# Sharing out the projection steps beside the attention by the number of keys of a unit

## The reference, cut to what matters

```python
proj = x @ w_in[l]                       # 1024 x 1024 tokens and channels, all branches' columns
q, k, v = ...                            # 8 heads of 64 channels
logf = jax.nn.log_sigmoid(c_f + b_forget[l])
cum = jnp.cumsum(logf, axis=1).transpose(0, 2, 1)
for i in range(seq // Q_BLOCK):          # 8 blocks of 128 queries
    q0, end = i * Q_BLOCK, (i + 1) * Q_BLOCK
    s = jnp.einsum('bqhd,bkhd->bhqk', q[:, q0:end], k[:, :end]) * scale
    s = jnp.where(causal, s + decay, -jnp.inf)
    p = jax.nn.softmax(s, axis=-1)
    outs.append(jnp.einsum('bhqk,bkhd->bqhd', p, v[:, :end]))
```

## Time and profile before

| what | value |
|---|---|
| median of 3 runs | 1223.13 us (1222.97 to 1225.02) |
| the profiled execution: its own time | 1223.87 us |
| the profiled execution: span in the trace | 1222.1 us |
| TensorE (PE) busy | 1203.0 us, 98% of the span, 5704 matmuls |
| VectorE (DVE) busy | 781.5 us, 64% |
| GpSimd (POOL) busy | 693.5 us, 57% |
| ScalarE (ACT) busy | 539.5 us, 44% |
| the four attention pairs | from 644.5 to about 935 us of the span |
| chain that ended last | PE 86%, DVE 7%, ACT 3%, issue 2%, DMA 1%, POOL 1% |

### The profile page before, as it was taken

One profiled execution on the slowest core, in us unless ns is written; L12 is line 12 of the kernel. 1 busy time (PEld: TensorE's weight loads), 2 busy tenths in 40 slices (PEclk: granted clock), 3 DMA queues, 4 the chain that ended last, 5 costly groups with the idle time before them and its releaser, 6 DMA issues.

```text
span 1222.1 us, 15758 instructions
## 1 busy us (share of the span) xinstructions
PE 1203.0 (98%) x5704; PEld 999.2 (82%) x5704; DVE 781.5 (64%) x1285; ACT 539.5 (44%) x992; POOL 693.5 (57%) x550
## 2 busy tenths in 40 slices
PE   7999999999999999999999999999999999999997
PEld 6888888888888888888888888888888888878886
DVE  4723765677566674438587665666666786876755
ACT  5433434344443443557354565656556444315000
POOL 5677887887777777777226444455533225547000
PEclk9999999999999999999999999999999999999999
DMA  8022131232323423234412111111002533376131
GB/s 278 1 69 69 35 104 35 69 138 101 106 105 103 138 104 104 104 105 148 162 53 56 32 53 52 35 53 46 24 18 92 191 111 116 105 260 241 66 130 69
DMA packets 91277, 118.61 MB, mean 97 GB/s; under 512 B 6072, under 2 KB 72632, under 8 KB 91200
## 3 DMA queue, kind: packets, MB, share of 16 engines
q1 hardware_dynamic: 91200, 117.60, 29.2%
HBM read 92.39 MB, written 25.20 MB: 96 GB/s over the span
## 4 chain that ended last, share of the span: by engine, by line
PE 86%; DVE 7%; ACT 3%; issue 2%; DMA 1%; POOL 1%; DVEq 0%; SPq 0%; ACTq 0%
PE pj L745 11%; PE pj L746 11%; PE pj L747 11%; PE pj L816 5%; PE pj L817 5%; PE pj L818 5%; PE pj L1074 4%; PE pt L746 3%; PE pt L747 3%; PE pt L745 3%; PE po L930 3%; PE pt L917 2%; PE po L1074 2%; PE pt L1074 2%; PE pj L833 2%
## 5 line engine op out<-in xcount | busy, mean ns | idle before, releaser
L1571 POOL TENSOR_TENSOR ring_lo<-w_pair,ring_hi 128x512 fp32r<-128x512 f32 x168 | 232.3, 1385 | 111.3 <-ACT ring_hi L1130 111.1
L1624 POOL TENSOR_TENSOR w_lo<-w_raw,w_hi 128x128 fp32r<-128x128 f32 (+1 forms) x104 | 111.2, 1088 | 161.6 <-ACT w_hi L1220 159.5
L1130 ACT ACTIVATE ring_hi<-w_pair 128x512 fp32r<-128x512 f32 x168 | 105.1, 628 | 160.6 <-PE pj L747 108.6
L1785 DVE SCALAR_TENSOR_TENSOR po<-glu,cwa,po 128x512 f32<-128x512 f32 x232 | 159.4, 747 | 20.6 <-ACT po L1181 20.6
L745 PE MATMUL pj<-t_hi,ring_hi 128*128 128x512 f32 x392 | 152.8, 390 | 0.3 <-DVE slot L1749 0.3
L746 PE MATMUL pj<-t_lo,ring_hi 128*128 128x512 f32 x392 | 152.5, 389 | 0.0
L747 PE MATMUL pj<-t_hi,ring_lo 128*128 128x512 f32 x392 | 152.5, 389 | 0.0
L816 PE MATMUL pj<-xT_hi,w_hi 128*128 128x512 f32 x320 | 126.5, 395 | 0.0
L817 PE MATMUL pj<-xT_lo,w_hi 128*128 128x512 f32 x320 | 125.4, 392 | 0.0
L818 PE MATMUL pj<-xT_hi,w_lo 128*128 128x512 f32 x320 | 125.0, 391 | 0.0
L1664 POOL TENSOR_SCALAR probs<-probs,rinv 128x128 f32<-128x128 f32 (+3 forms) x32 | 57.9, 1810 | 110.8 <-DVE rinv L2103 110.8
(11 more groups left out here) (344 smaller groups left out, 2952.1 us busy)
## 6 DMA issues: line engine op xcount, KB each, us to landing
w_pair<-in_w_in SPq DMA_DIRECT2D x28, 1024.0 KB, 5.2
gate_scratch<-slot SPq DMA_DIRECT2D x16, 1024.0 KB, 4.0
gate<-gate_scratch SPq DMA_DIRECT2D x32, 512.0 KB, 3.8
w_raw<-in_w_in SPq DMA_DIRECT2D x20, 512.0 KB, 3.9
z_scratch<-slot SPq DMA_DIRECT2D x8, 512.0 KB, 2.6
bias<-cum_scratch SPq DMA_DIRECT2D x8, 512.0 KB, 3.8
wout_raw<-in_w_out SPq DMA_DIRECT2D x8, 512.0 KB, 5.5
x_tok<-in_x SPq DMA_DIRECT2D x8, 512.0 KB, 4.3
```

What stands on the lines that cost most here:

```text
L1130: nc.scalar.activation(ring_hi[:, j % RING, :, :], w_src(u, p), ACT.Copy).then_inc(s_rhi, 1)
L1571: nc.gpsimd.tensor_tensor(ring_lo[:, j % RING, :, :], w_src(u, p), ring_hi[:, j % RING, :, :], ALU.subtract).then_inc(s_rlo, 1)
L1624: nc.gpsimd.tensor_tensor(w_lo[:, j % 2, k, :], w_raw[:, j % 2, k, :], w_hi[:, j % 2, k, :], ALU.subtract).then_inc(s_wlo, 1)
L1785: nc.vector.scalar_tensor_tensor(out=acc if n < PAD_A else src, in0=src, scalar=cwa[:, ct, n:n + 1], in1=acc, op0=ALU.mult, op1=ALU.add).t ...
```

## The change

A table gives every unit its number of steps, small where the unit has few keys and large where it has many, the same for both heads of the pair. Everything that was tied to "four steps a unit" is derived from the table: where the steps of a unit begin (FILL_AT), which unit takes out half n (EVAC_AT) and which unit splits the next weight tile (SPLIT_AT).

```diff
+        FILL_N = (2, 3, 3, 4, 4, 5, 5, 6) * 2
+        FILL_AT = [sum(FILL_N[:u]) for u in range(UNITS + 1)]
+        EVAC_AT = [next(u for u in range(UNITS + 1) if FILL_AT[u] >= KT * (n + 1)) for n in range(8)]
+        SPLIT_AT = [next(u for u in range(UNITS + 1) if FILL_AT[u] >= 2 * KT * n) for n in range(4)]
...
             def pair(c, last):
                 s = 4 * c
                 for u in range(UNITS):
-                    cut = 4 * u + (3 if u < 2 else 2)
+                    cut = FILL_AT[u] + (FILL_N[u] + 1) // 2
                     if u == 1:
                         turn_v(c)
-                    stream_part(s + S_C, S_C, 4 * u, cut)
+                    stream_part(s + S_C, S_C, FILL_AT[u], cut)
...
-                    stream_part(s + S_C, S_C, cut, 4 * u + 4)
+                    stream_part(s + S_C, S_C, cut, FILL_AT[u + 1])
...
-                    if k % 4 == 0:
-                        split_w(2 * c, 4 + k // 4)
+                    if k in SPLIT_AT:
+                        split_w(2 * c, 4 + SPLIT_AT.index(k))
...
-                    h = k // 2 % 2 ^ 1
-                    if k in (2, 4):
-                        raw_half(s + 3, h, q_raw, QSCALE)
...
-                    if k == 14:
-                        evac_half(s + 6, 0, 0, ACT.Tanh, 0.5)
+                    if k in EVAC_AT[:7]:
+                        n = EVAC_AT.index(k)
+                        h = n % 2
+                        if n < 2:
+                            raw_half(s + 3, h, q_raw, QSCALE)
...
+                        else:
+                            evac_half(s + 3 + n // 2, h, h, ACT.Tanh, 0.5)
...
-                    if k == 14:
+                    if k == EVAC_AT[6]:
                         gate_half(0, sg, 2 * c + 2 * last)
```

More of the change, by code:

```diff
@@ L1430, in pair @@
                             k_hi(a, range(2 - a))
-                    h = k // 2 % 2 ^ 1
-                    if k in (2, 4):
-                        raw_half(s + 3, h, q_raw, QSCALE)
[L1434 to L1439, removed]
-                    if k == 14:
-                        evac_half(s + 6, 0, 0, ACT.Tanh, 0.5)
+                    if k in EVAC_AT[:7]:
[3 more added lines that the diff above has]
+                            raw_half(s + 3, h, q_raw, QSCALE)
+                        elif n < 4:
+                            raw_half(s + 4, h, k_raw, QSCALE if last else 1.0)
+                        elif n < 6 and not last:
+                            raw_half(s + 5, h, v_raw, 0.5)
+                        else:
+                            evac_half(s + 3 + n // 2, h, h, ACT.Tanh, 0.5)
                 turned_hi(c, UNITS - 1)
@@ L1672, in pair @@
                         normalise(c, k + 1)
-                    if k % 4 == 0:
-                        split_w(4 * c + 4 + k // 4, 4 + k // 4)
+                    if k in SPLIT_AT:
+                        split_w(4 * c + 4 + SPLIT_AT.index(k), 4 + SPLIT_AT.index(k))
                     if k == 2 and c:
@@ L2153, in pair @@
                         q_lo(1, q_raw, q_stack, stk + 2)
-                    h = k // 2 % 2 ^ 1
-                    if k in (10, 12) and last:
-                        gate_half(h, v_raw, 2 * c)
-                    if k == 14:
+                    if k in EVAC_AT[4:6] and last:
+                        gate_half(EVAC_AT.index(k) % 2, v_raw, 2 * c)
+                    if k == EVAC_AT[6]:
                         gate_half(0, sg, 2 * c + 2 * last)
```

## The result

| | before | changed |
|---|---|---|
| median of 6 runs | 1223.34 us (1222.50 to 1225.02) | 1228.77 us (1227.22 to 1229.19) |
| ratio | | 1.0039 [1.0027, 1.0052] |
| profiled execution, its own time | 1223.87 | 1227.22 |
| its span | 1222.1 | 1225.4 |
| attention, start of the first scores to start of the memory's scores | 293.89 | 299.22 |

The changed kernel is slower by 5.4 us, 0.39%. Its profiled execution is the fastest of its runs, so the two spans lie only 3.3 us apart. The stretch that the change touches shows the whole of it. Two rows of TensorE's timeline bound this stretch, first in the kernel before, then in the changed one. A row is: start, length shown, engine, line, instruction, out<-in, tile, shape, count, and in brackets the idle time ahead of it and what ended that.

The account below looks back on a forecast made before the run. TensorE, busy 98% of the span, was taken as the bound, so only its standing counted. Terms -5.4 + 0.3 + 1.1 + 4.2 + 5.1 gave +5.3, a median of 1228.4 us; range 1226.0 to 1231.0, 8 in 10 1222.5 to 1232.0.

Parts of the forecast that it names:

- The sixteen waits go: Units 5, 7, 13 and 15 of all four pairs: `turn` no longer waits for VectorE's rests, -5.4 us.
- Unit 13/14 of the last pair: Last pair: VectorE waits in unit 13 for gate half 5 behind a weight tile's split, +0.3 us once.
- Start of pair 0: Units 0 and 1 lose two steps ahead of the second half of `turn_v`, so TensorE stands there, +1.1 us.
- Boundary: Between pairs, three times: gate half 6 lengthens the ScalarE and VectorE chain to 11.0 us, +1.4 each, +4.2 us.
- Units 1 to 4: Every pair: two fewer steps become standing at `turn` of unit 4, 1.4 in pairs 1 to 3, 0.9 in pair 0, +5.1.
- The scaling at 2.91 us: Unit 4: GpSimd's scaling of 640 columns still takes 2.91 us behind k_lo, against 1.8 alone.
- the light units cost nothing: Rival: the two steps taken from units 1 to 4 weren't needed; sum +0.2, 1223.3 us; chance 0.16.
- The chain at the boundary has play: Rival: gate half slips in at +0.4 each and units 1 to 4 close up; -2.8, 1220.3 us; chance 0.09.
- More places turn late: Rival: slack in units 11 and 12 gone, unit 2's scaling collides, or half the waits stay; at most 1232.7 us; chance 0.15.

Follow-up runs that it names:

- gate_half_early: Changed kernel with gate half 6 taken out in unit 14, as before the change, instead of unit 15; 1224.76 us, ratio 1.0011 to the kernel before.
- cuts_567: Kernel before, four steps in every unit, with three ahead of `turn` also in units 5, 6 and 7 of each head; 1218.78 us, ratio 0.9965.
- k_rest_later: Changed kernel with VectorE's two k_lo of units 2 and 3 moved to units 4 and 5; 1223.72 us, ratio 1.0003 to the kernel before.
- cuts_only: Kernel before, four steps in every unit, with three ahead of `turn` also in units 5, 7, 13 and 15; 1222.59 us, ratio 0.9993.
- cuts_567_split_later: `cuts_567` with the first weight tile of a pair split in unit 2 instead of unit 0, on ScalarE and GpSimd; 1226.95 us, ratio 1.0028.
- uneven_all_mended: Changed kernel with gate half 6 in unit 14, k_lo in units 4 and 5, first weight tile split in unit 2; 1223.47 us, ratio 0.9999.

## Why the prediction was right, point by point

- *The sixteen waits go, -5.4.* They all went; no place in units 5 to 7 and 13 to 15 of the first three pairs stands.
- *Unit 13/14 of the last pair, +0.3.* Measured 0.50, and 0.21 at unit 12, which I had as free with 0.3 of slack: 0.7 in place of 0.3.
- *Start of pair 0, +1.1.* 0.59 + 0.57 less the 0.15 of before is 1.0. The place was half right: I had all of it in `turn_v` (about 0.8), but 0.59 stand a unit earlier, at the scores of unit 2, which wait for VectorE's reading of unit 1.
- *Boundary, 3 x 1.4.* 0.49 + 1.41 - 0.45 = 1.45 each. The chain was to be 11.0 us and is 11.16; the product was to start 3.60 after the high parts of unit 14 and starts 3.63 after. `gate_half_early` takes 3.5 of it back by moving this one half, so without it in the chain that much is gone; the remaining 0.36 in `turn_v` is TensorE arriving earlier, as `cuts_567`, with no half 6 in the chain, shows too (0.81 as well).
- *Units 1 to 4, 5.1.* Measured 3 x 1.39 + 0.60 = 4.8. The sum was right, its places were not: I named only the wait of `turn` in unit 4, which was to be 0.9 to 1.5 us in every pair and is 0.48 to 0.63; another 0.78 stands one unit earlier, where the scores of unit 5 wait for VectorE's reading of unit 4's. I had listed that row of VectorE's queue as a link of the chain to the scaling and not asked who waits for it directly. In pair 0 the two steps cost 0.6 and not 0.9.
- *The scaling at 2.91 us.* It took 2.91 wherever k_lo stands directly ahead of it (units 4), 2.77 where k_lo had started 0.18 before it (unit 12 of pairs 0 to 2), and 1.89 where none does: unit 12 of the last pair in both kernels, and every unit 4 of `k_rest_later`. The estimate for it alone was 1.8. That agrees with the rule cited from the Trainium skill (SBUF — State Buffer, "Who interferes with whom"): the added 1.02 us is most of k_lo's 1.22.

```profile
916.14 1.89 POOL L1672 TENSOR_SCALAR probs<-probs,rinv 128x640 f32<-128x640 f32 x1 [4.91 <-DVE rinv L2111]
```

The terms are off by +0.4 (last pair), -0.1 (start of pair 0), +0.1 (boundary) and -0.3 (units 1 to 4), and these cancel. That the sum came within 0.1 us of the measured 5.4 is in part luck, the more so as the interval of the ratio leaves anything from 3.3 to 6.4 us; that each term has the right sign and nearly its size isn't.

The rivals: "the light units cost nothing" fell with the waits of units 3 and 4, 4.8 us where it has none. "The chain at the boundary has play" fell with 11.16 us against the 9.6 at which it would have decided. "More places turn late" came true only in the last pair: 0.2 at unit 12 and 0.2 more than forecast at unit 14.

What was weak, and showed only in the experiments: the thought that a step put ahead of a wait costs nothing behind it. Three expectations rested on it or on its like: `cuts_only` on the steps of TensorE, `cuts_567_split_later` and `uneven_all_mended` on ScalarE's queue, with GpSimd's left uncounted.

## What to carry to other kernels

Filler work in a tuned stream is a budget between two waits, not a thing with a best average: giving more of it to the heavy units took it from the light ones, where other engines had just as much to do. First move the cut between "ahead of the wait" and "behind it" inside each unit, which here gave 4.4 us with one line, and look at the next wait down the line each time. Before moving an operation on one engine, write down the queues of all engines that carry a part of it, up to the next thing that TensorE waits for.

## What the runs showed of the hardware

**The clock behind a standing.** TensorE had been busy without a gap (8.00 of 8.00 us up to 733), stood 2.27 us, and then had a granted clock of 0.57 over 4 us; from 739.5 on it was 1.00 again. Of three such standings two had this, though TensorE was as busy ahead of each (8.00 of 8.00 us). Behind a standing of 1.4 us in the changed kernel it stayed at 1.00, in the stretch around `turn_v`:

```profile
720.50:724.50 4.00, 3.50 (x19) 2.95 (x20) 3.00 (x6) 2.18 (x6) 3.04 (x4) 1.00 0.31 86
```

So a wait can cost more than its length, here 1.5 us more. Why the third standing had no such tail is open.

**VectorE and GpSimd beside each other.** It goes in both directions, and each time the one that started later is the longer one. k_lo, 1.22 us alone, took 2.84 beside GpSimd's product z of 2.40 that had started 0.64 before it, and the scaling took 2.91 in place of 1.89 beside k_lo. In the first case 0.64 + 2.84 = 3.48 is close to the two lengths one after the other, 2.40 + 1.22 = 3.62.
